# Stick-breaking scores of the first mixer from high and low fp32r parts

## The reference, cut to what matters

```python
def block(args):
    qb, n = args
    z = jnp.einsum('bhqd,bhsd->bhqs', qb, kh).astype(jnp.float32) * (S_DH ** -0.5)
    tpos = n * S_BLOCK + jnp.arange(S_BLOCK)
    strict = kpos[None, :] < tpos[:, None]
    log_keep = jnp.where(strict, jax.nn.log_sigmoid(-z), 0.0)
    suffix = lax.cumsum(log_keep, axis=log_keep.ndim - 1, reverse=True) - log_keep
    a = jnp.where(strict, jnp.exp(jax.nn.log_sigmoid(z) + suffix), 0.0)
    return jnp.einsum('bhqs,bhsd->bhqd', a.astype(vh.dtype), vh)
```

## Time and profile before

| | us |
|---|---|
| median of 3 runs | 3086.13 |
| lowest and highest run | 3083.64, 3088.2 |
| the profiled execution | 3087.61 |
| its span, first to last instruction | 3085.9 |
| window attention, first to last scores of its kind | 448.3 to about 557 |
| stick-breaking attention, first scores to end of values | 557.3 to 673.3 |
| mean granted TensorE clock | 0.967 |

### The profile page before, as it was taken

The page is one execution under the profiler, slowest core; times in us unless marked ns, Lnnn a source line. Parts: engine busy times, 40 slices in busy tenths (PEclk is TensorE's granted clock), DMA queues, the critical chain, the costliest instruction groups (busy, mean ns, idle before and its releaser), DMA issues.

```text
span 3085.9 us, 39346 instructions
## 1 busy us (share of the span) xinstructions
PE 2931.9 (95%) x15355; PEld 2354.5 (76%) x15355; DVE 2011.8 (65%) x3446; ACT 1152.2 (37%) x1949; POOL 75.2 (2%) x152
## 2 busy tenths in 40 slices
PE   3999999999998999899999999989988999999999
PEld 3868875565787888677888888868857788888887
DVE  5444205557535556648777778769995787777785
ACT  3234215442314555524333334441134433333444
POOL 1000000110040000000000000000000000000000
PEclk7999999999999999799999999999998999999999
DMA  8010210012210000123333356321102333334633
GB/s 311 21 31 21 62 28 18 18 55 70 82 31 8 1 1 1 55 89 96 109 110 109 115 201 214 100 58 48 35 9 68 108 111 109 110 109 170 227 98 103
DMA packets 180756, 256.26 MB, mean 83 GB/s; under 512 B 29368, under 2 KB 131676, under 8 KB 176220
## 3 DMA queue, kind: packets, MB, share of 16 engines
q1 hardware_dynamic: 176432, 228.25, 22.5%
q10 hardware_dynamic: 4139, 25.50, 2.0%
HBM read 186.62 MB, written 67.11 MB: 82 GB/s over the span
## 4 chain that ended last, share of the span: by engine, by line
PE 86%; DVE 8%; ACT 2%; issue 1%; DMA 0%; DVEq 0%; ACTq 0%
PE ps L1513 26%; PE ps L1521 14%; PE ps L1468 10%; PE ps L1071 3%; PE ps L1326 3%; PE ps L1416 3%; PE ps L1084 3%; PE ps L1108 3%; PE ps L950 2%; PE ps L1238 2%; PE ps L1218 2%; PE ps L1263 2%; PE ps L1398 2%; PE ps L1380 2%; PE ps L1577 2%
## 5 line engine op out<-in xcount | busy, mean ns | idle before, releaser
L1513 PE MATMUL ps<-x_ops,w_ring 128*128 128x512 f32 x3696 | 840.3, 389 | 6.3 <-ACT even_rows L2118 3.2
L1513 PEld LDWEIGHTS ps<-x_ops,w_ring 128*128 128x128 f32 x3696 | 693.3, 188 | 151.4 <-issue 7.9
L1521 PE MATMUL ps<-a_ring,w_ring 128*128 128x512 f32 x1848 | 419.5, 389 | 0.0
L1521 PEld LDWEIGHTS ps<-a_ring,w_ring 128*128 128x128 f32 x1848 | 346.8, 188 | 72.4 <-DVE w_ring L2837 0.5
L1468 PE MATMUL ps<-h_high,ring_parts 128*128 128x512 f32 x1024 | 320.3, 394 | 18.0 <-DVE h_low L2342 9.3
L2060 ACT ACTIVATE w_ring<-ring 128x512 fp32r<-128x512 f32 x230 | 144.1, 628 | 300.7 <-PE ps L1513 284.8
L1468 PEld LDWEIGHTS ps<-h_high,ring_parts 128*128 128x128 f32 x1024 | 193.4, 190 | 64.1 <-issue 13.5
L2351 DVE TENSOR_TENSOR ring_parts<-ring,ring_parts 128x1024 fp32r<-128x1024 f32 (+1 forms) x65 | 81.1, 1250 | 203.9 <-ACT ring_parts L1715 203.5
L1468 PE MATMUL ps<-h_low,ring_parts 128*128 128x512 f32 x512 | 200.7, 392 | 0.0
L2837 DVE TENSOR_TENSOR w_ring<-ring,w_ring 128x512 fp32r<-128x512 f32 x230 | 158.1, 688 | 38.7 <-ACT w_ring L2060 38.7
L2073 ACT ACTIVATE a_ring<-a_raw 128x512 fp32r<-128x512 f32 x150 | 94.5, 630 | 207.2 <-PE ps L1521 169.6
(11 more groups left out here) (462 smaller groups left out, 4689.4 us busy)
## 6 DMA issues: line engine op xcount, KB each, us to landing
a_raw<-act_kept SPq DMA_DIRECT2D x70, 512.0 KB, 3.8
act_kept<-even_rows SPq DMA_DIRECT2D x12, 1536.0 KB, 5.1
act_kept<-odd_rows SPq DMA_DIRECT2D x10, 1536.0 KB, 5.1
ring<-in_ffn_w_gate_dram SPq DMA_DIRECT2D x12, 1024.0 KB, 5.8
ring<-in_ffn_w_up_dram SPq DMA_DIRECT2D x12, 1024.0 KB, 6.1
ring<-in_conv_w_pw_dram SPq DMA_DIRECT2D x24, 512.0 KB, 3.8
late<-in_ffn_w_gate_dram SPq DMA_DIRECT2D x10, 1024.0 KB, 5.9
late<-in_ffn_w_up_dram SPq DMA_DIRECT2D x10, 1024.0 KB, 6.1
```

Of the source, the lines that this page charges most:

```text
L1513: last = mm(o, w_ring[:, i % 4, wp_, P * k:P * k + P], x_ops[:, X_OP[p], rp_, k, :], start=p in "176" and k == 0 and p_ == 0, stop=k == 3 ...
L1521: last = mm(bank(OUT_BANK[DOWN_GROUP[p] + c_]), w_ring[:, (A_UNITS + b) % 4, wp_, P * c_:P * c_ + P], a_ring[:, b % 4, rp_, :], start=p in ...
```

## The change

The stick-breaking scores are computed in fp32r from parts. For each head, `q_stack` holds on 128 rows the high part of the queries (on the head's own 64 rows) and the low part (on the other 64); `k_double` holds the high part of the keys twice, on both halves; `sk_low` holds the low part of the keys, written over `sk`, on the head's rows. One product on 128 rows gives high by high plus low by high, and a second one on 64 rows adds high queries by low keys.

ACT writes the high parts of the queries out of PSUM, one head at a time, and DVE the low parts, in the stage "attention_in". The keys' parts are made beside the attention: ACT's `keys_doubled` and DVE's `keys_split`, for heads 0 and 1 in whole at window units 16 and 24 (DVE two steps later), for heads 2 and 3 in halves, 512 keys after the last window unit and 512 at stick-breaking units 4 and 8. PE waits for `k_split` ahead of each head's first unit, and again in block 4 for heads 2 and 3. The pieces of the diff below stand in the order: placements, units, PE's attention loop, ACT's part of attention_in and its two loops, the same for DVE.

```diff
-        sq = place("sq", [P, 2, S], 4 * 3072)
+        sk_low = place("sk_low", [P, 2, S], 4 * 1024, F32R)
+        q_stack = [place("q_stack%d" % h, [P, S], o_, F32R)
+                   for h, o_ in enumerate((12288, 16384, 20480, A_BIG + 4 * 13312))]
+        k_double = [place("k_double%d" % h, [P, S], A_BIG + 4 * o_, F32R) for h, o_ in enumerate((20480, 21504, 9216, 10240))]
...
-                    "stick", i, h, sq[rows_of(half), c_, P * i:P * i + P], sk[rows_of(half), c_, 0:w], w,
+                    "stick", i, h, q_stack[h][:, P * i:P * i + P], k_double[h][:, 0:w], w,
                     lambda b, h=h: sv[:, b, 64 * h:64 * h + 64]))
+                stick_units[-1].q_high = q_stack[h][rows_of(half), P * i:P * i + P]
+                stick_units[-1].k_low = sk_low[rows_of(half), c_, 0:w]
...
+        K_EARLY, K_LATE = (16, 24), (4, 8)
...
+                        if un.kind == "stick" and un.i == 0:
+                            pe.wait_ge(s.k_split, un.h + 1)
+                        elif un.kind == "stick" and un.i == 4 and un.h >= 2:
+                            pe.wait_ge(s.k_split, un.h + 3)
                         for a in range(0, un.w, 512):
                             e = min(512, un.w - a)
-                            last = mm(ps[:, o + a:o + a + e], un.q, un.k[:, a:a + e], start=True, stop=True)
+                            last = mm(ps[:, o + a:o + a + e], un.q, un.k[:, a:a + e], start=True, stop=un.kind == "swa")
+                            if un.kind == "stick":
+                                last = mm(ps[:, o + a:o + a + e], un.q_high, un.k_low[:, a:a + e], start=False, stop=True)
...
-            for i in range(2):
-                copy_out(J_ATT + 10 + i, [cp(sq[:, i, :], sc_=w8)])
+            for h in range(S_H):
+                j = J_ATT + 10 + h // 2
+                a.wait_ge(s.g_out, j + 1)
+                rows = rows_of(h % 2)
+                f(q_stack[h][rows, :], bank(2 * (j % 2), 2)[rows, :], ACT.Copy, scale=w8).then_inc(s.q_high, 1)
+            def keys_doubled(h, c0, c1):
+                rows, other = rows_of(h % 2), rows_of(1 - h % 2)
+                f(k_double[h][rows, c0:c1], sk[rows, h // 2, c0:c1], ACT.Copy)
+                f(k_double[h][other, c0:c1], sk[rows, h // 2, c0:c1], ACT.Copy).then_inc(s.k_high, 1)
...
+                    if i in K_EARLY:
+                        keys_doubled(K_EARLY.index(i), 0, S)
+                    elif i >= N:
+                        keys_doubled(2 + i - N, 0, S // 2)
...
+                if i in K_LATE:
+                    keys_doubled(2 + K_LATE.index(i), S // 2, S)
...
+            for h in range(S_H):
+                j = J_ATT + 10 + h // 2
+                rows, other = rows_of(h % 2), rows_of(1 - h % 2)
+                v.wait_ge(s.q_high, h + 1)
+                ins = stt(q_stack[h][other, :], bank(2 * (j % 2), 2)[rows, :], A_D ** -0.5, q_stack[h][rows, :].bitcast(F32),
+                          mul, sub)
+                if h % 2:
+                    ins.then_inc(g_free[j % 2], 1)
+            def keys_split(h, c0, c1, count):
+                rows = rows_of(h % 2)
+                v.wait_ge(s.k_high, count)
+                tt(sk_low[rows, h // 2, c0:c1], sk[rows, h // 2, c0:c1], k_double[h][rows, c0:c1].bitcast(F32), sub)\
+                    .then_inc(s.k_split, 1)
...
+                    if i - 2 in K_EARLY:
+                        keys_split(K_EARLY.index(i - 2), 0, S, K_EARLY.index(i - 2) + 1)
+                    elif i >= N + 2:
+                        keys_split(i - N, 0, S // 2, i - N + 1)
...
+                    if i - 2 in K_LATE:
+                        keys_split(2 + K_LATE.index(i - 2), S // 2, S, 5 + K_LATE.index(i - 2))
```

More of the change, by code:

```diff
@@ L240, in build @@
         s.par_in = sem("par_in")
-        s.x_in = sem("x_in")
+        s.x_qk_in = sem("x_qk_in")
         s.small_in = sem("small_in")
@@ L325, in build @@
         s.ym_copied = sem("ym_copied")
-        s.qk_in = sem("qk_in")
+        s.k_split = sem("k_split")
         s.mvg_in = sem("mvg_in")
@@ L734, in _ @@
                 load(big[:, 4096 * half:4096 * half + 4096].rearrange("p (t d) -> p t d", d=D),
-                     x[0].rearrange("(t p) d -> p t d", p=P)[:, 4 * half:4 * half + 4, :], s.x_in)
+                     x[0].rearrange("(t p) d -> p t d", p=P)[:, 4 * half:4 * half + 4, :], s.x_qk_in)
             def load_mod(k):
@@ L766, in _ @@
             load(mvg_raw.rearrange("p (k n) -> p k n", k=KC), win_v[:, :, C_MVG:C_MVG + VGW], s.mvg_in)
-            load(qk[:, 0], m_wq[0].rearrange("h d e -> d h e"), s.qk_in)
-            load(qk[:, 1], m_wk[0].rearrange("h d e -> d h e"), s.qk_in)
+            load(qk[:, 0], m_wq[0].rearrange("h d e -> d h e"), s.x_qk_in)
+            load(qk[:, 1], m_wk[0].rearrange("h d e -> d h e"), s.x_qk_in)
             for h in range(2, M_H):
@@ L967, in _ @@
             pe.wait_ge(s.const_ok, 2)
-            pe.wait_ge(s.x_in, 32)
+            pe.wait_ge(s.x_qk_in, 32)
             for k in range(KC):
@@ L1124, in queries_keys @@
                 else:
-                    pe.wait_ge(s.qk_in, 32)
+                    pe.wait_ge(s.x_qk_in, 64)
                     pe.wait_ge(s.cu_ok, M_H)
@@ L1698, in root @@
                 f(root_sum, ps[:, 3072:3072 + TB], ACT.Sqrt, bias=eps, scale=1.0 / D).then_inc(s.rs_ready, 1)
-            a.wait_ge(s.x_in, 32)
+            a.wait_ge(s.x_qk_in, 32)
             for t in range(TB):
@@ L2660, in queries_low @@
                 src = bank(2 * (j % 2), 2)
-                v.wait_ge(s.q_high, 2 * i + 1)
+                v.wait_ge(s.q_high, S_H + 2 * i + 1)
                 stt(qt[64:128, i, :], src[0:64, :], N_D ** -0.5 / n_slope(i), qt[0:64, i, :].bitcast(F32), mul, sub)
-                v.wait_ge(s.q_high, 2 * i + 2)
+                v.wait_ge(s.q_high, S_H + 2 * i + 2)
                 stt(qt[0:64, 4 + i, :], src[64:128, :], N_D ** -0.5 / n_slope(i + 4), qt[64:128, 4 + i, :].bitcast(F32),
@@ L2670, in keys_low @@
                 src = bank(2 * (j % 2), 2)
-                v.wait_ge(s.k_high, count)
+                v.wait_ge(s.k_high, 6 + count)
                 for g in range(2):
```

## The result

The changed kernel takes 3094.16 us (median of 20 executions), the kernel before 3086.14 beside it. The ratio is 1.0027, with a 95% interval from 1.0021 to 1.0033: slower by 0.27%, 6.5 to 10.2 us. One execution of the changed kernel took 3585.76 us at a mean clock of 0.765; it is a disturbed one, and the ratio leaves it out (the median of the other 19 is 3094.03). The profiled execution took 3095.2 us, its span is 3093.4 and its mean clock 0.966.

The account below looks back on a forecast made before the run. PE was taken as the bound, fully busy in both attentions. Terms -2.7 + 2.5 + 2.0 + 0.4 = +2.2 us on the profiled 3087.61 gave 3089.8, or 3088.3 for the median; range 3080 to 3093.

Parts of the forecast that it names:

- Part 1: Stick-breaking scores on PE: 15.4 us less streaming, 64 more row-count changes at 0.20 us cost 12.8; net 2.7 us off.
- Rival A: Stick-breaking scores: no stall between row counts, so starts 0.23 apart and the kernel at 3077.3 us; chance 0.12.
- Part 2: End of attention_in: making the queries' parts on ACT and DVE delays the window attention 2.5 us, bounds 2.3 to 2.7.
- Part 3: Behind PE's longer pause, at the window attention's start: about 4 us at half clock lose 2.0 us, bounds 0 and 3.4.
- Part 4: Keys' copies and subtractions on ACT and DVE beside the attentions: 0.4 us more, bounds 0 and 1.5.
- B: Slower rival: clock falls to 0.50 for a third of the 59.4 us stick-breaking stretch, 10 us more, 3098; chance 0.06.
- C: Slower rival: inserted low-part copies hit PE in full, 4 x 1.5 us, in the window attention; 3093.9; chance 0.04.

Follow-up runs that it names:

- rows128: Changed kernel with the second score product also on all 128 rows (adds low-by-low terms of another head): 3080.61 us, ratio 0.9982.
- grouped: Changed kernel with score products of units over 512 keys ordered 128, 128, 64, 64 rows instead of 128, 64, 128, 64: 3092.06 us, ratio 1.0008.
- before_pause: Kernel before plus two spare additions on VectorE at the end of attention_in, making a longer PE pause: 3092.75 us, ratio 1.0021.
- keys_only: Kernel before with all the keys' parts made but unused, scores still f32, no PE wait on k_split: 3086.12 us, ratio 1.0000.
- swap: Changed kernel with the queries' columns projected ahead of the keys', so one copy follows the last product: 3086.69 us, ratio 0.9995.
- after_again: The changed kernel, unedited, timed and traced a second time against the kernel before: 3093.95 us, ratio 1.0022.
- warm: Changed kernel plus four idle f32 products on PE in the pause behind its last projection product: 3088.67 us, ratio 1.0003.
- pause_warm: Kernel before plus two spare VectorE additions making a pause and four idle PE products inside it: 3090.19 us, ratio 1.0005.
- warm_rows128: Changed kernel with both score products on 128 rows and four idle PE products in the pause: 3068.46 us, ratio 0.9948.
- swap_rows128: Changed kernel with queries projected ahead of keys and both score products on 128 rows: 3071.15 us, ratio 0.9950.

## Why the prediction was wrong

It forecast 3088.3 us, no change, with a range of 3080 to 3093. It came out at 3094.16.

**Part 1, the score products: right.** Forecast 2.7 us off, a full-width unit at about 4.23 us and starts about 0.41 apart; the trace shows 2.4 off, 4.29, and 0.43. The 1.65 and 4.23 were a slip of the sum: 0.80 us saved in streaming less 0.60 for three changes is 0.20, so a group of 1.72 and a unit of 4.30, which is what came. For width 128 the two products and their seam take 0.51 us (564.25 to 564.76) instead of 0.41, the small loss that was forecast. That the row count is what decides, and not the accumulation or the wait, `rows128` shows: same products, same columns, 0.23 apart. The price of 0.20 a change, taken from f32 products on 4 rows, held for 64 rows in fp32r: 0.20 by `grouped`. The Trainium skill, TensorEngine Tiling (Array Packing), Key Properties, says that a changed tiling mode drains the engine. The trace agrees, with 0.20 us as the price, which the sum had by rows. Rival A is refuted.

**Part 2, the pause: right.** Forecast 2.5 us, measured 2.50.

**Part 3, the clock behind it: right in kind, too small, and this is the step that failed.** The prediction took the 3.5 us at 0.51 in the earlier trace rows as the length of such a stretch: "A half-speed stretch of about 4 us loses some 2 us", with an upper bound of 3.4 for seven microseconds. It was the length of one case. Behind the five pauses of about 3.6 us in the profiled executions of this work (the changed kernel twice, `before_pause`, `grouped`, `rows128`) the clock stayed at 0.50 for 6.8, 6.8, 6.8, 3.4 and 23.9 us, and in the traces that cost 2.8, 2.8, 2.9, 1.7 and 11.2 us, a mean of 4.3. By medians it is 5.5, between 2 and 9. So the term should have been 4 to 5.5 with an upper bound near 11, instead of 2.0 and 3.4. The two traces of the changed kernel itself have 2.8 and lie inside the bound; the pairs of medians don't. The kernel before had the warning: in the earlier trace rows a stretch of five microseconds is at 0.50 throughout, with PE busy all the time. Its trace has 24 stretches at 0.50, of 3.0 to 30.7 us, seven of them over 10 us. One of 17.1 us, in the windows view of the kernel before:

```profile
1289.50:1306.50 17.00, 14.73 (x55) 11.29 (x54) 7.75 (x39) 8.58 (x23) 0.00 (x0) 0.50 0.47 186
```

That such a stretch can be far longer than four microseconds was there to be read.

**Part 4, the keys' parts: right.** Forecast 0.4 us, bounds 0 and 1.5; `keys_only` measured 0 (2.5 less to 2.8 more), and the traces of the changed kernel and of `swap` show 0.1 in the window attention. No wait on `k_split` held PE: its gaps in the two attentions are those of the kernel before.

**The sum with the measured terms** is -2.4 + 2.5 + 5.5 + 0.1 = +5.7 us, against 6.8 (3.4 to 10.2) for `after_again` and 8.3 (6.5 to 10.2) for the first measurement. Of what is left, 1.1 to 2.6 us, the place in the later layer takes 0.4 to 0.9, a term that the prediction didn't have; the remainder lies within what these runs can tell and isn't explained. The timed executions carry no trace, but each has a mean granted clock, and the spread goes with it: the fastest of the changed kernel (3084.43) has 0.968, the two slowest (3100.53, 3100.57) 0.961 and 0.962, against 3082.05 to 3089.20 us for the kernel before. That it is the stretch behind the pause that varies is argued, not shown, and between kernels this mean doesn't sort the times: `swap` has 0.966 on average at 3086.69 us.

**The rivals.** B said that the clock would fall inside the stick-breaking attention. It stayed at 1.00 there (57 of 57 us), with the row counts alternating all the way, so B is refuted; what the clock goes by, no run here shows. C fell with `keys_only`: that its 3093.9 lies 0.3 us from the measured time is a coincidence. No rival had the price of part 3 as its one mechanism: the case that decided was the forecast's own, with a longer stretch.

**The range.** It took in each upper bound singly. Part 3's upper bound as the traces now show it, 11.2 us and so 9.2 above the value taken, would have carried it to 3097.5, and past the point from which the change is slower.

## What to carry to other kernels

Count the changes of row count that an edit puts between products, not only its columns: here half of 30.7 us of streaming was saved, and 64 changes at 0.20 us gave most of it back (12.8 of 15.3 us); sorting the products by row count and moving the preparation off the end of the stage made the same idea 5.9 us faster than before. A pause of PE costs its own length and then the clock, and that second price is a spread and not a number: take it from several stretches at half clock in the profile, or fill the pause with idle products (where there was no long pause they only cost). A trace of one execution holds such stretches at chance places, so read an edit's gain in its own stretch, and the whole by many runs.

## What the runs showed of the hardware

The length of the stretch at half clock behind one and the same pause was 3.4, 6.8 or 23.9 us, with PE busy in nearly all of it (4.00 of 4.00 us in the windows from 448 to 468 of `rows128`). The Trainium skill, TensorE: Matmul & The Clock Gate, Part 1, says that the clock's recovery is run-variable, with the same kernel showing different counts of slow products; the runs agree, and the longest stretch here, 23.9 us with a cost of 11.2, is far from negligible in a comparison of 0.3%. Idle products of 3.17 us inside the pause kept the clock at 1.00 in the three kernels that had them there (`warm`, `pause_warm`, `warm_rows128`).

A change from 128*64 to 128*128, with the row count kept, costs about 0.11 us at its first product (0.34 against 0.23 in `rows128`), half of what a change of row count costs. The type changes there too, from f32 to fp32r; no run tells the two apart.

POOL's masks took longer in the kernels whose PE ran faster: 24.58 us of 58 in `swap_rows128` against 8.90 of 57 in the changed kernel. One pair of them took 0.54 us in the changed kernel and up to 1.78 there. A single mask with no DVE instruction beside it took 0.29 us in both (median); 42 of the 76 in `swap_rows128` overlap one, with a median of 0.45, against 5 of 65 in the changed kernel. That DVE is the cause isn't shown.
